# GpSimd in place of VectorE for the low parts of the u tiles, in the 48 steps with one-hot matrices

## The reference, cut to what matters

```python
def peer_ffn(h, w_query, sub_keys, expert_u, expert_v):
    qry = (h @ w_query).reshape(T, P_HEADS, 2, P_HALF)
    scores = jnp.einsum("thcd,hcnd->thcn", qry, sub_keys)
    s_top, i_top = lax.top_k(scores, P_TOPK)
    ...
    best_s, best_pos = lax.top_k(cand_s, P_TOPK)
    expert_idx = jnp.take_along_axis(cand_i, best_pos, axis=-1)
    gates = jax.nn.softmax(best_s, axis=-1)
    ...
        act = jax.nn.gelu(jnp.einsum("td,thkd->thk", hb, expert_u[eb]), approximate=False)
        return jnp.einsum("thk,thkd->td", act * gb, expert_v[eb])
```

## Time and profile before

| | |
|---|---|
| time, median of 3 runs | 2015.2 us |
| lowest and highest | 2012.47 and 2019.03 us |
| profiled execution, span from the first to the last instruction | 2011.3 us |
| TensorE busy | 1937.0 us, 96% |
| VectorE busy | 1489.4 us, 74% |
| ScalarE busy | 719.0 us, 36% |
| GpSimd busy | 481.5 us, 24% |
| one-hot products (L2016), first and last start | 1107.6 and 1389.1 us |

### The profile page before, as it was taken

How to read it: one execution, slowest core, us unless ns; L and a number is a source line. 1 busy time by engine, 2 the same in 40 slices (tenths; PEclk the granted TensorE clock), 3 DMA queues, 4 the chain that set the end, 5 groups by cost and what they waited for, 6 DMA issues and landing times.

```text
span 2011.3 us, 27895 instructions
## 1 busy us (share of the span) xinstructions
PE 1937.0 (96%) x10341; PEld 1714.5 (85%) x10341; DVE 1489.4 (74%) x2727; ACT 719.0 (36%) x1324; POOL 481.5 (24%) x240
## 2 busy tenths in 40 slices
PE   5999998999999989999999999999999999999998
PEld 3889776889877888899999999999988888888886
DVE  5677445364475545787889999997689889899895
ACT  4110234010252243344443444444444444444443
POOL 0443202343213113100111521111222323332221
PEclk9999999999999999999999999999999999999999
DMA  6335511354212422257767688888999999999993
GB/s 253 105 106 182 172 54 48 106 191 147 63 43 73 158 80 88 72 173 255 234 225 241 231 318 297 299 296 300 412 395 401 401 400 398 400 398 401 400 375 115
DMA packets 212642, 467.99 MB, mean 233 GB/s; under 512 B 13576, under 2 KB 157120, under 8 KB 193344
## 3 DMA queue, kind: packets, MB, share of 16 engines
q1 hardware_dynamic: 194112, 332.54, 47.6%
q0 software_dynamic: 18432, 134.23, 16.9%
HBM read 412.19 MB, written 54.53 MB: 232 GB/s over the span
## 4 chain that ended last, share of the span: by engine, by line
PE 52%; DVE 2%; DMA 2%; ACT 1%; issue 0%; POOLq 0%; POOL 0%; SPq 0%; ACTq 0%; DVEq 0%
PE xin_out L2038 26%; PE xin_ps_u L1994 22%; PE xin_out L2016 4%; DMA con_raw<-in_expert_u 2%; DVE in_ulo L2156 1%; ACT in_uhi L2067 0%; DVE experts_rows L1787 0%; DVE experts_acc L1806 0%; DVE over_s_stage L2170 0%; ACT L2109 0%; ACT over_v_vhi L2074 0%; DVE over_v_vlo L2305 0%; POOLq L95 0%; POOL xin_x L2147 0%; DVE over_s_stage L2253 0%
## 5 line engine op out<-in xcount | busy, mean ns | idle before, releaser
L1780 POOL DMA_INDIRECT experts_rows<-in_expert_rows,experts_idx x128 | 247.3, 1932 | 873.2 <-DVE experts_acc L1806 738.4
L1994 PE MATMUL xin_ps_u<-con_h_hi,in_uhi 128*128 128x384 f32 x1024 | 349.0, 341 | 9.4 <-DVE in_ulo L2156 7.2
L1994 PE MATMUL xin_ps_u<-con_h_hi,in_ulo 128*128 128x384 f32 x1024 | 343.3, 335 | 0.0
L1994 PE MATMUL xin_ps_u<-con_h_lo,in_uhi 128*128 128x384 f32 x1024 | 343.3, 335 | 0.0
L2038 PE MATMUL xin_out<-over_v_vhi,xin_whi 128*128 128x512 f32 x768 | 239.1, 390 | 2.1 <-DVE xin_wlo L2307 2.0
L2038 PE MATMUL xin_out<-over_v_vhi,xin_wlo 128*128 128x512 f32 x768 | 238.8, 390 | 0.0
L2038 PE MATMUL xin_out<-over_v_vlo,xin_whi 128*128 128x512 f32 x768 | 238.5, 390 | 0.0
L2156 DVE TENSOR_TENSOR in_ulo<-con_raw,in_uhi 128x1024 fp32r<-128x1024 f32 x127 | 155.5, 1224 | 78.3 <-ACT in_uhi L2067 75.9
L488 POOL TENSOR_TENSOR weights_wlo<-con_raw,weights_whi 128x2048 fp32r<-128x2048 f32 x32 | 147.5, 4609 | 251.9 <-DVE weights_whi L561 251.9
L1994 PEld LDWEIGHTS xin_ps_u<-con_h_hi,in_uhi 128*128 128x128 f32 x1024 | 193.1, 189 | 13.7 <-DVE in_ulo L2156 11.1
L1994 PEld LDWEIGHTS xin_ps_u<-con_h_lo,in_uhi 128*128 128x128 f32 x1024 | 193.2, 189 | 0.0
(11 more groups left out here) (344 smaller groups left out, 3742.4 us busy)
## 6 DMA issues: line engine op xcount, KB each, us to landing
con_raw<-in_expert_u SPq DMA_DIRECT2D x128, 512.0 KB, 4.7
con_raw<-in_expert_v SPq DMA_DIRECT2D x128, 512.0 KB, 12.0
con_raw<-in_w_in SPq DMA_DIRECT2D x38, 1024.0 KB, 6.0
act_scratch<-in_act SPq DMA_DIRECT2D x128, 192.0 KB, 2.4
experts_hot<-act_scratch SPq DMA_DIRECT2D x128, 192.0 KB, 11.8
gate_scratch<-in_stage SPq DMA_DIRECT2D x12, 1024.0 KB, 7.1
gate_scratch<-over_s_stage SPq DMA_DIRECT2D x12, 1024.0 KB, 7.7
experts_hot<-gate_scratch SPq DMA_DIRECT2D x16, 768.0 KB, 14.1
```

The lines of the kernel that those rows point to most:

```text
L1780: pool.indirect_dma_start(out=self.rows[:, r % ROWS, :], out_offset=None, in_=table, in_offset=at).then_inc(self.row_in[r % ROWS], 16)
L1994: mm = pe.matmul(ps_u[s % 2][:, 0:TD], a[s % 2][:, k, :], m[:, k, P:T], start=(i == 0), stop=(i == 3 * KD - 1))
```

## The change

In the 48 steps 60 to 107, `cut(n + 1)`, the subtraction that makes ulo of tiles 61 to 108, is issued by GpSimd instead of VectorE, with the same operands. Both engines count up the same semaphore `lo_done`; GpSimd's first one waits until VectorE's earlier ones are done, and VectorE's first one after the stage waits until GpSimd's are. GpSimd's program, which was a plain list of 128 fetches, now follows the steps: in step n it issues the subtraction (if it is one of the 48) and then the fetches that take the buffers of the rows of step n − 2. These were added in step n − 1, so that a fetch that could go out at the add goes out behind the next step's subtraction.

```diff
--- before.py
+++ after.py
@@ -1818,6 +1818,9 @@
 FIRST_LOADS = N_HOT0 + N_HOT + 14
 
 
+HOT_CUTS = range(N_HOT0 + 1, N_HOT0 + N_HOT + 1)
+
+
 def slots_of_steps():
 
 
@@ -2127,11 +2130,26 @@
 
         @block.gpsimd
         def _(pool):
+            def cut(n):
+
+                if n == HOT_CUTS[0]:
+                    pool.wait_ge(lo_done, n)
+                pool.wait_ge(hi_done, n + 1)
+                pool.tensor_tensor(ulo[n % 2][:], cut_of[n % U_RING], as_f32(uhi[n % 2][:]), ALU.subtract).then_inc(lo_done, 1)
+
             pool.wait_ge(got.idx_done, 1)
-            for r in range(ROWS):
+            r = ROWS
+            for i in range(ROWS):
+                got.fetch(pool, i, A["expert_rows"])
+            for n in range(NEXP):
+                if n + 1 in HOT_CUTS:
+                    cut(n + 1)
+                for added in IN_AT[n - 2] if n > 1 else []:
+                    got.fetch(pool, r, A["expert_rows"])
+                    r += 1
+            while r < SLOTS:
                 got.fetch(pool, r, A["expert_rows"])
-            for r in range(ROWS, SLOTS):
-                got.fetch(pool, r, A["expert_rows"])
+                r += 1
             pool.wait_ge(ms0_done, 1)
             pool.tensor_tensor(rstd0[:], ms0[:], con.pow_half[:, 0:1], ALU.pow).then_inc(pow0_done, 1)
             def power(t):
@@ -2152,6 +2170,8 @@
         def _(dve):
             def cut(n):
 
+                if n - 1 == HOT_CUTS[-1]:
+                    dve.wait_ge(lo_done, n)
                 dve.wait_ge(hi_done, n + 1)
                 dve.tensor_tensor(ulo[n % 2][:], cut_of[n % U_RING], as_f32(uhi[n % 2][:]), ALU.subtract).then_inc(lo_done, 1)
 
@@ -2316,7 +2336,7 @@
                     dve.wait_ge(slots_done, ND)
                 if N_HOT0 <= n < N_HOT0 + N_HOT:
                     gates(n - N_HOT0)
-                if n < NEXP - 1:
+                if n < NEXP - 1 and n + 1 not in HOT_CUTS:
                     cut(n + 1)
                 if n < N_SEARCH:
                     rt.search(dve, PH - LATE_HEADS + n // PIECES, n % PIECES)
```

## The result

| | before | changed |
|---|---|---|
| time, median (lowest to highest) | 2014.15 us (2012.47 to 2019.03), 4 runs | 2060.16 us (2059.57 to 2063.06), 4 runs |
| span of the profiled execution | 2011.3 us | 2057.8 us |

The changed kernel takes 1.0228 times as long, 95% interval 1.0212 to 1.0243: 46 us slower, where 40 were forecast. The prediction named 2055 us, in a range of 2040 to 2105. (Its base of 2015.2 us was the median of the first three of these four runs of the kernel before.)

The account below looks back on a forecast made before the run. TensorE was taken to set the 48 steps at 5.95 us; GpSimd's blocking would make VectorE's step 6.78. The 0.83 us more in each of 48 steps gives +40 on 2015.2, 2055 us, range 2040 to 2105.

Parts of the forecast that it names:

- Who sets the step: In the 48 steps before the change: TensorE sets 5.95 us, VectorE needs 5.71 and has 0.24 of slack.
- The price of a subtraction: In the 48 steps: each GpSimd subtraction blocks VectorE's two-SBUF-input operations, costing VectorE 2.2 us, between 2.02 and 2.40.
- startup passing while it stands: At the blocked VectorE operation: 0.14 us of its startup passes during the block, so it ends 1.08 after GpSimd.
- at its word (+49): In the 48 steps: the skill's blocking rule read literally, 2.40 us lost per subtraction, sums to +49 us.
- 48 steps at 6.78: VectorE's step becomes 4.58 + 2.20 = 6.78 us; TensorE waits 0.83 per step, 40 us in all.
- Nothing is made up behind the stage: After the 48 steps: TensorE, 90% busy or more up to the last slice, has no pause that could shrink.
- SyncE's lead of three steps: At the u tile loads: a subtraction ending 2 us later takes that from a lead of some 18 us.
- What would show it: In the 48 steps' timeline: one-hot products every 6.8 us, some 40 us of TensorE idle time before them.
- Late port: In the 48 steps: subtractions wait long for the port, up to 5.28 us; +85 to some +110; chance 0.28.
- limit of 3.4: In the 48 steps: a GpSimd subtraction's wait for the port is free up to 3.4 us.
- No conflict: In the 48 steps: broadcast inputs leave the port free, TensorE keeps 5.95, kernel 2015 less 0.4; chance 0.09.
- half of it: In the 48 steps: only some subtractions hit VectorE's work, +6 to +28 us, around 2030; chance 0.08.

Follow-up runs that it names:

- e10: The kernel before with a gathered row in every one of the 48 steps in place of every second; 2061.49 us, ratio 1.0228.
- e5: The changed kernel with only every second of the 48 subtractions on GpSimd, the others on VectorE; 2033.24 us, ratio 1.0092.
- e7: The kernel before, with GpSimd also making two 512-column subtractions per step that nobody reads; 2111.52 us, ratio 1.0478.
- e1: The changed kernel with the one-hot operations taking index table and gates from PSUM; 2020.0 us, ratio 1.0024.
- e3: The kernel before with only the changed kernel's fetch order, each fetch waiting for `lo_done`; 2015.97 us, ratio 1.001.
- e9: e1 with a gathered row in every one of the 48 steps in place of every second; 2024.15 us, ratio 1.0044 against the kernel before.
- e8: The kernel before, with GpSimd also making two 512-column memsets per step, which read nothing; 2014.68 us, ratio 0.9998.
- e6: The changed kernel with each GpSimd subtraction made twice in a row into the same tile; 2167.12 us, ratio 1.0759.
- e2: The kernel before with index table and gates for the one-hot operations in PSUM, subtractions on VectorE; 2015.38 us, ratio 1.0001.

## Why the prediction was right

- **Who sets the step.** "TensorE sets the step at 5.95, and VectorE has 0.24 us of slack": e10 confirms it, one operation more on VectorE makes a step of 6.87.
- **The price of a subtraction.** 2.2 us was taken between 2.02 and 2.40; the step of the changed kernel gives 2.20, e5 to e7 2.18, 2.24 and twice 1.11. The detail of the count holds nearly, and by two deviations that cancel: GpSimd works 2.32 us after VectorE's end (1203.94 to 1206.26) where 2.23 was counted, and the blocked operation ends 1.02 us after GpSimd where 1.08 was counted; 2.32 + 1.02 − 1.14 is 2.20. That it ends less than its usual 1.13 after GpSimd is measured; that this is startup passing while it stands is the prediction's reading and wasn't tested. By the rule of the Trainium skill, "SBUF — State Buffer", section "Who interferes with whom", as the prediction took it at its word (+49), the stage would have lost 8 us more than the 41.2 it lost.
- **48 steps at 6.78.** 46 steps measured 6.780, so 48 × 0.83 = 40 stands. The stage lost 41.2: its first step and its last lost 1.6 and 1.7 in place of 0.83. The other 5 us of the 46 are outside the sum: 3.0 at the stage's end, 1.0 behind the first loop, and 1.3 by which its first loop starts later, within what the profiles vary by.
- **"Nothing is made up behind the stage"** was right in its sign, but the stage's end was costed at nothing and lost 3.0: the u loads queue behind the last gates on SyncE, and the same load took 10.34 us in place of 7.47. The prediction's sentence on SyncE's lead of three steps didn't see that at this place the lead is used up, in the kernel before too. Why this load takes 3 us longer in the changed kernel is not settled; the transfer engines are full during it in both, 1.00 and 0.98 of the time. e1 has the long load as well (10.49), e3 less (8.46, TensorE's waits 5.8), which points to the fetches' places, but e3's time can't be told from the kernel before.
- **What would show it.** "One-hot products every 6.8 us", one VectorE operation a step at "some 3.3" (3.40), the others 1.21 to 1.27, GpSimd's subtraction 2.73 and 3.08: as forecast. TensorE's waits are before the one-hot products, 34.5 us of the "some 40".
- **The rivals.** *Late port*: in the changed kernel the fetches of the stage take 1.76 or 1.77 us, none 6.22, and each subtraction waits for at most the rest of one VectorE operation (the longest record is 3.39 us). e5's subtractions wait for more, and what decides how long GpSimd waits stays open: the prediction set this rival aside because most fetches had waited for one operation at most, and that the subtractions of the changed kernel did the same was in part luck. A wait of e5's 2.05 us would have been free by the prediction's own limit of 3.4. *No conflict* and *half of it*: the one-hot operations with repeated inputs are hit like the others, 3.40 for L2314 (and 3.37 for a comparison, L2310, in e5). They became true only in e1, where an operand moved to PSUM.

## What to carry to other kernels

Moving an operation from VectorE to GpSimd doesn't take it off VectorE when both sides read two SBUF tiles: count nearly GpSimd's whole time for it as VectorE's (2.2 of 2.4 us here, against the 1.13 saved), and compare the sum with the engine that sets the step. Where one operand of VectorE's can live in PSUM, the two engines do run side by side; the move then costs the stage's steps nothing (e1), but is worth something only if the room is used for other work, as e9 does. A stall at the border of two stages can be an ordering of one transfer queue and a shortage of bandwidth at once: here fixing one of the two moved it or left it, and fixing both removed it.

## What the runs showed of the hardware beyond that

- GpSimd's memsets of 512 columns cost VectorE nothing (e8), its subtractions of 512 columns 1.11 us each (e7).
- A fetch that starts during a VectorE operation with two SBUF inputs mostly takes until 0.9 us after that operation's end: in the changed kernel the dot is over at 1207.28 and the fetch at 1208.18, in e6 a one-hot comparison (L2314) at 1205.82 and the fetch at 1206.72. In e2, where they start beside one-hot operations that read one operand from PSUM, all 22 between 1119 and 1380 take 0.94. The rows of e6's comparison and its fetch, and e2's fetches as a group:

```profile
1202.52 3.37 DVE L2314 TENSOR_TENSOR experts_hot<-con_iota,in_slot 128x1024 f32<-128x1024 f32 x1
```
```profile
1204.96 1.76 POOL L1780 DMA_INDIRECT experts_rows<-in_expert_rows,experts_idx  x1
```
```profile
L1780 POOL DMA_INDIRECT experts_rows<-in_expert_rows,experts_idx x22 | 20.6, 937 | 238.9 <-DVE experts_acc L1806 238.9
```

The Trainium skill, "SBUF — State Buffer", section "Who interferes with whom", infers that a `tensor_tensor` on VectorE leaves the generation of transfer descriptors on GpSimd alone; for these fetches the rows disagree, by 1.76 (e6) against 0.94 us (e2). Each of them also takes its row numbers from an SBUF tile (`experts_idx`); whether that or the descriptors is what waits isn't shown.
- Why five fetches of the kernel before waited for five VectorE operations in a row (6.22 us), and none of the changed kernel for more than one, though VectorE has fewer pauses there, stays open, as does why e5's subtractions waited for two. Waits like the 6.22 would have been the worst case of the prediction.
